# Picks sent to their units by SyncE, the streams' states one in a step, and the step sizes' products in the norm's last steps

## The reference

```
h = rmsnorm(x, ln1_w) * (1 + sc1) + sh1
proj = h @ w_in;  z, xbc, dt, lx, ly, g_ssd, g_lru = split(proj)
xbc = silu(causal_conv(xbc));  dt = softplus(dt + dt_bias)
y, ssd_h_new = ssd_scan(xs, dt, -exp(a_log), bm, cm, h0)     # chunked state space scan
y_ssd = rmsnorm(y * silu(z));  y_lru = rglru(conv(lx)) * gelu(ly)
x = x + g1 * ((sigmoid(g_ssd) * (y_ssd @ w_br_ssd) + sigmoid(g_lru) * (y_lru @ w_br_lru)) @ w_out)
h = rmsnorm(x, ln2_w) * (1 + sc2) + sh2
q = h @ wq;  128 experts per token by two top-16 searches over 128 keys, then a top-16 of the sums
x = x + g2 * sum_k gelu(h . u[e_k]) * g_k * v[e_k]
```

## Time and profile before

| | us |
|---|---|
| median of 3 runs | 4614.37 |
| lowest and highest | 4608.49, 4616.39 |
| the profiled execution: its own time | 4609.44 |
| its span, first to last instruction | 4607.7 |
| mean granted TensorE clock | 0.799 |

### The profile page before, as it was taken

How to read it: one execution, slowest core, us unless ns; L and a number is a source line. 1 busy time by engine, 2 the same in 40 slices (tenths; PEclk the granted TensorE clock), 3 DMA queues, 4 the chain that set the end, 5 groups by cost and what they waited for, 6 DMA issues and landing times. The chain is left out here.

```text
span 4607.7 us, 60395 instructions
## 1 busy us (share of the span) xinstructions
PE 3212.4 (70%) x21986; PEld 1895.2 (41%) x21986; DVE 2825.9 (61%) x6591; ACT 1466.3 (32%) x4657; POOL 1436.5 (31%) x1298
## 2 busy tenths in 40 slices
PE   7899994777777664488999864767777664444443
PEld 4455552445454442254555431445555442121111
DVE  2422058695864587676743696965854587675454
ACT  2224012443622222333722222433622222232222
POOL 0000003333334334323333323334334334344332
PEclk8999996878888776589999875778888786555555
DMA  7333328899999999968999978999999999999998
GB/s 320 142 147 101 101 82 320 343 356 379 417 417 419 419 400 396 413 265 311 382 380 378 366 292 364 395 364 406 418 418 419 420 404 390 421 420 421 421 422 336
DMA packets 279860, 1610.83 MB, mean 350 GB/s; under 512 B 56410, under 2 KB 61328, under 8 KB 112524
## 3 DMA queue, kind: packets, MB, share of 16 engines
q0 software_dynamic: 184320, 1342.26, 71.6%
q1 hardware_dynamic: 65808, 255.49, 14.5%
q10 hardware_dynamic: 29436, 9.24, 0.8%
HBM read 1597.63 MB, written 7.91 MB: 348 GB/s over the span
## 5 line engine op out<-in xcount | busy, mean ns | idle before, releaser
L528 POOL DMA_INDIRECT ring<-in_peer_uv,units x1280 | 1433.3, 1120 | 3136.3 <-PE psum L923 2219.9
L1827 DVE SCALAR_TENSOR_TENSOR ring<-ring,hrow 128x1024 f32<-128x1024 f32 x1280 | 1538.4, 1222 | 890.7 <-DMA ring<-in_peer_uv,units 864.3
L923 PE MATMUL psum<-ring,diag 128*32 128x256 f32 x10240 | 926.0, 495 | 1182.9 <-ACT diag L1292 1181.9
L541 PE MATMUL psum<-hT,wslot 128*128 128x384 f32 (+1 forms) x4224 | 1283.0, 461 | 27.7 <-DMA wslot<-in_w_tiles 24.6
L541 PEld LDWEIGHTS psum<-hT,wslot 128*128 128x128 f32 x4224 | 845.7, 205 | 456.9 <-issue 111.1
L923 PEld LDWEIGHTS psum<-ring,diag 128*32 128x32 f32 x10240 | 322.2, 131 | 1705.1 <-ACT diag L1292 1394.1
L1282 ACT ACTIVATE gel<-hid 128x2 f32<-128x2 f32 x640 | 129.1, 202 | 1935.5 <-DVE ring L1827 1881.0
L541 PE MATMUL psum<-region,wslot 128*128 128x384 f32 (+1 forms) x1536 | 446.8, 446 | 5.5 <-DVE xT L1682 2.2
L541 PEld LDWEIGHTS psum<-region,wslot 128*128 128x128 f32 x1536 | 293.8, 195 | 152.0 <-issue 28.2
L1292 ACT ACTIVATE diag<-pick,wgt 128x32 f32<-128x32 f32 x1280 | 331.7, 306 | 0.0
L1286 ACT ACTIVATE wgt<-gel,units 128x1 f32<-128x1 f32 x1280 | 307.4, 287 | 20.9
(11 more groups left out here) (247 smaller groups left out, 2806.0 us busy)
## 6 DMA issues: line engine op xcount, KB each, us to landing
wslot<-in_w_tiles SPq DMA_DIRECT2D x360, 512.0 KB, 7.7
ring<-in_w_modt SPq DMA_DIRECT2D x24, 2048.0 KB, 9.0
ring<-in_peer_uv,units POOLq DMA_INDIRECT x1280, 13.7
wslot<-in_w_gate SPq DMA_DIRECT2D x32, 128.0 KB, 9.6
region<-in_states_t SPq DMA_DIRECT2D x16, 256.0 KB, 13.2
region<-in_states_n SPq DMA_DIRECT2D x16, 256.0 KB, 10.0
out_new_ssd_sample<-region ACTq DMA_DIRECT2D x16, 256.0 KB, 15.4
xT<-in_x_t SPq DMA_DIRECT2D x1, 2560.0 KB, 8.9
```

The source lines that it names most:

```text
L528: pool.indirect_dma_start(ring[:, n, :], None, table, bass.IndirectOffsetOnAxis(ap=units[:, s % 2, block, 0, quad:quad + 1].bitcast(U32), ...
L541: last = pe.matmul(out, wslot[:, n % SLOTS, k * P:(k + 1) * P], src(k), start=k == 0, stop=k == KT - 1)
L923: last = pe.matmul(psum[c * BLOCK:(c + 1) * BLOCK, block % 2, block // 2 * 256:(block // 2 + 1) * 256], diag[:, n, :], ring[:, n, D + c * ...
L1827: dve.scalar_tensor_tensor(out=ring[:, n, 0:D], in0=ring[:, n, 0:D], scalar=1.0, in1=hrow[:, e % 2, :], op0=ALU.mult, op1=ALU.mult, accum_ ...
```

## The change

SyncE walks the same plan. It issues weight loads up to four tiles past those that the entries so far have used, and issues the picks' DMAs at the entries where ACT did. The last three `states_n` loads stand behind the first three LX tiles. The eight states are added, scaled and written one in a step instead of two. On PE the products of the step sizes for prompt tiles stand in N1's steps 6 to 9, two rows of h in each, as these become `modulated`; those of the streams' tile stay in X0.

```
+                ahead, taken = weights(), 0
+                for e, steps in PLAN:
+                    while n < min(taken + SLOTS, REGIONS * LOADS):
+                        next(ahead)
+                    if e and e[0] < TILES_E and same_group(e[0]) and e[1] == choice_at(e[0]) + 28:
+                        spread(e[0] + 1, 0)
+                    for r, i in steps:
+                        if r < REGIONS:
+                            taken += loads_in(r, i)
+                            if r == 0 and i == BASE[0]["Q"] + 13:
+                                spread(0, 0)
+                            if i == BASE[r]["Q"] + 21:
+                                spread(TILE0[r], passes(TILE0[r]) - 1)
...
-                        if g and j == 4:
-                            states(l)
+                            if g and j == 4:
+                                states(l, range(13))
+                            yield load(tile(l, TZ + j))
...
+                        for j in range(8):
+                            yield load(tile(l, TLX + j))
...
+                            if g and j < 3:
+                                states(l, (13 + j,))
...
+                def spread(s, h):
+                    sp.wait_ge(E["ready"], s + h + 1 if s == 0 else s + 2)
+                    if s >= 2:
+                        sp.wait_ge(E["wgt"], (s - 1) * UNITS)
+                    c = slice(h * length(s), (h + 1) * length(s)) if s == 0 else slice(0, QUADS)
+                    for block in range(BLOCKS):
+                        for r in range(BLOCKS):
+                            sp.dma_start(units[r * BLOCK:(r + 1) * BLOCK, s % 2, block, :, c],
+                                         picked[block * BLOCK:(block + 1) * BLOCK, s % 2, r, :, c]).then_inc(E["spread"], 16)
...
 # PE
+                def steps_of_dt(lay, u, k):
+                    return pe.matmul(bank(7)[:, u * HEADS:(u + 1) * HEADS], hT[:, k, lay.t0 + u * P:lay.t0 + (u + 1) * P],
+                                     wdt[:, k * HEADS:(k + 1) * HEADS], start=k == 0 and u == 0, stop=k == KT - 1, skip_group_check=True)
...
+                    if -6 <= i < -2:
+                        if i == -6:
+                            pe.wait_ge(S["mean"], at("mean", 2 * r))
+                            pe.wait_ge(loaded["wdt"], 16 * (l + 1))
+                        pe.wait_ge(S["modulated"], at("modulated", 2 * r, 2 * i + 13))
+                        for k in (2 * i + 12, 2 * i + 13):
+                            for u in range(lay.nt - lay.sample):
+                                last = steps_of_dt(lay, u, k)
+                        if i == -3 and not lay.sample:
+                            last.then_inc(S["dt_mm"], 1)
...
 # PE, DVE and ACT, the streams' states (9, 10 and 11 are steps of the tile's scan)
-                    if 9 <= i <= 12:
+                    if 9 <= i <= 16:
+                        j = i - 9
...
-                    if s and 10 <= i <= 13:
+                    if s and 10 <= i <= 17:
+                        j = i - 10
...
-                        if 11 <= i <= 14:
+                        if 11 <= i <= 18:
+                            j = i - 11
...
 # ACT
-                    if r == 0 and i == 13:
-                        spread(0, 0)
-                    if i == 21:
-                        spread(s, passes(s) - 1)
...
-                        if p == choice_at(s) + 28:
-                            spread(s + 1, 0)
```

More of the change, by code:

```diff
@@ L163, with loads_in @@
 POS = weight_positions()
+LOADS = 98
+TILE0 = [NT * (r // 2) + FIRST[r % 2] for r in range(REGIONS)]
+def loads_in(r, i):
+    return sum(each for name, count, each in (("X", 10, 1), ("Z", 8, 1), ("LX", 8, 1), ("LRU", 8, 2), ("M", 32, 1), ("OUT", 8, 1), ("Q", 16, 1))
+               if 0 <= i - BASE[r][name] < count)
 PER = {"zeroed": 2, "sampled": 2, "modset": 3, "zscaled": 8, "xfill": 18, "conved": 18, "tapped": 18, "kept": 18, "xth": 10, "silued": 10, "acb": 2, "ea": 2, "seg": 4, "e": 4, "w": 2, "y": 2, "ys": 2,
@@ L431, in small_ones, with states @@
                     sp.dma_start(kT[:], a["keys"].rearrange("p (l i k) -> p l i k", l=DEPTH, i=2)[:, l, :, :]).then_inc(loaded["keys"], 16)
-                def states(l):
+                def states(l, loads):
                     lay = G[1]
-                    for i in range(16):
+                    for i in loads:
                         slot = i % 5
@@ L482, in _ @@
+                for _ in ahead:
+                    pass
             @block.gpsimd
@@ L589, in x_stage @@
                             pe.wait_ge(S["sampled"], at("sampled", l, 0))
-                        pe.wait_ge(S["mean"], at("mean", 2 * r))
-                        pe.wait_ge(loaded["wdt"], 16 * (l + 1))
-                        for u in range(lay.nt):
                             for k in range(KT):
[L594 to L597, removed]
+                                last = steps_of_dt(lay, lay.nt - 1, k)
+                            last.then_inc(S["dt_mm"], 1)
                     if 0 <= i < 10:
@@ L1293, in diagonals @@
                            .then_inc(E["diag"], 1)
-                def spread(s, h):
-                    act.wait_ge(E["ready"], s + h + 1 if s == 0 else s + 2)
-                    if s >= 2:
-                        act.wait_ge(E["wgt"], (s - 1) * UNITS)
-                    c = slice(h * length(s), (h + 1) * length(s)) if s == 0 else slice(0, QUADS)
-                    for block in range(BLOCKS):
-                        for r in range(BLOCKS):
-                            act.dma_start(units[r * BLOCK:(r + 1) * BLOCK, s % 2, block, :, c],
-                                          picked[block * BLOCK:(block + 1) * BLOCK, s % 2, r, :, c]).then_inc(E["spread"], 16)
                 def take_out(o):
```

93 lines of the change are left out of this document (44 added, 49 removed).

## The result

| | us |
|---|---|
| before, median of 4 runs | 4611.43 (4608.39 to 4616.39) |
| after, median of 4 runs | 4584.81 (4583.61 to 4585.75) |
| ratio after/before, 95% interval | 0.9943 (0.993 to 0.9955) |
| after, the profiled execution and its span | 4585.02, 4583.3 |

The change saves 24 to 27 us, 0.6%. The forecast was 4586 us. The sum is right; several of its terms are not, and they cancel, which is in part luck. This part shows where the time came from, place by place.

The account below looks back on a forecast made before the run. Gathers set the pace wherever the DMA engines move 417 to 422 GB/s. Terms -5, -3.7, -4, -14, -3 and +3 sum to -26.7 us, from 4609.4 to 4583 (4588 against the median); forecast 4586 us, its own range 4573 to 4602.

Parts of the forecast that it names:

- The bound: Whole run: gathers set the pace at 417 to 422 GB/s; an edit gains only DMA time given back elsewhere.
- Step sizes in region 2: Region 2's norm and X0: products follow ACT two rows at a time, X0 ends earlier; -5 us.
- Region 0: Region 0's products: PE starts at 42.5 instead of 46.2, passes end at 52.9 instead of 56.6; -3.7 us.
- Regions 1 and 3: Norm and X0 there: 16 of 32 passes move, 3.5 us each, counted 2 us each; -4 us, bounds -7 and +6.
- The picks: Picks leave ACT for SyncE, at tile 0, tile 5 and other sets; -14 us together, bounds -22 and 0.
- 7.5 us for a set is my estimate: SyncE's issue of a set of picks, from five state loads at 0.47 us each, against ACT's 10.5 us.
- the 3 at the start: First half of tile 0's picks: the first gather can start 3 us earlier (0 to 6).
- Weights behind the picks: SyncE's weight loads behind each set of picks: issues and landing fit the cover of 20 to 30 us; 0.
- States in region 1: States one in a step, late loads behind LX tiles; DVE still waits 5 to 10 us; -3 us, bounds -10 and +8.
- States in region 3: State loads behind tile 6's picks, PE waits 10 to 16 us at S11; +8, so +3 with the gain.
- More comes back: Rival, 20%: ring covers S11 in region 3, no DVE wait in region 1, N1 waits free; -47 us, 4567.
- The slower rival: Rival, 10%: weights come late behind the picks, 15 us at each of four sets; +33 us, 4647.

Follow-up runs that it names:

- E1: Kernel before with only the step sizes' products moved into the norm's last steps; 4597.53 us, ratio 0.9974.
- E2: Kernel before with only the picks issued by SyncE along the plan, states two in a step, all loads at Z4; 4598.53 us, ratio 0.9970.
- E4: Changed kernel with the step sizes' products back in X0; 4595.18 us, ratio 0.9965.
- E5: Changed kernel with the first five state loads of a region issued right behind the load of Z3, ahead of tile 6's picks; 4580.53 us, ratio 0.9936.
- E6: Changed kernel with tile 1's picks three plan entries later, behind region 1's last two state loads; 4578.06 us, ratio 0.9929.
- E8: Changed kernel with tile 1's picks three and tile 6's fifteen entries later, behind the last state loads of their region; 4568.67 us, ratio 0.9918.
- E10: E8 with the step sizes' products of regions 1 and 3 back in X0; 4570.63 us, ratio 0.9921.
- E3: Kernel before with only the states one in a step and their last three loads behind LX tiles; 4602.93 us, ratio 0.9988.
- E11: E8 with states two in a step and all 16 loads at Z4, as before; 4577.65 us, ratio 0.9936.
- E12: E9 with each state written as 128 rows of 2 KB, not 1024 of 256 bytes, in other output places; a probe only; 4562.58 us, ratio 0.9898.
- E9: E8 with the first half of tile 0's picks issued half by SyncE and half by ACT; 4567.53 us, ratio 0.9913.

## Why the prediction was right, and where its steps were not

- **The bound.** Reading the price of an edit from the GB/s of its own stretch held: the saturated stretches gave nothing (unit 128 to 384: 14.3 to 15.7), and the dips gave all.
- **Step sizes in region 2: -5, measured -6.5 (E1) to -8.3.** The mechanism is as told, group by group behind ACT, with the pair's sums behind them. The last product ends 3.2 us after ACT's last row, for 2.6. But the terms differ. PE gains 5.4 us up to X0's end, of which 1.8 are X0 at a higher clock, a term that the forecast did not have. X0's start was forecast 14.0 us behind ACT's first row (1961.5 - 1947.5) and came at 15.3: the step that was mis-sized is the pair's sums and the turning, put at about 3 us together, which took 3.5 (1942.9 to 1946.4), and the last product, put 11.3 us behind ACT's first row and measured at 11.8. Without the clock the gain would have been 3.6. E2 to E4, with the old code, gain 0.9 to 1.7 by the lead here too, so of the 6.5 some 5 are left; and of the 8.3 up to unit 464 the last 1.6 are in neither E1, E5, E6 nor E8 (-0.5 to 0.0).
- **Region 0: -3.7, measured 3.5** between ACT's and PE's starts, 4.2 in the lead and 4.0 between the means of the kernels with and without it.
- **Regions 1 and 3: -4, measured about 0 in the changed kernel.** The step that failed is "I count 2 us each": 3.5 us of passes left X0, but the rest of the products, with the pairs' sums now between them, end no sooner. In region 3 X0 starts 14.8 us behind ACT's first row and before 14.6, in region 1 13.5 and 13.3. From unit 656 to 704, which holds region 3's N1, the lead is 26.7 and 27.0. In region 1 four kernels of nine got 3 to 4 us, with the clock at 1.00 in X0 (told with E10); the forecast did not have that either.
- **The picks: -14, measured -14 (E2), by other terms.** The step that failed is "7.5 us for a set is my estimate" (tile 0's halves took 10.3 and 10.8, tile 1's and tile 6's sets 11.8 and 11.4): five state loads in a row were the wrong neighbour for transfers of another form, and ACT's own row, which I had as the bound, was the truth. That takes away the 3 at the start. The second half of tile 0 gave 8 rather than 5, and tile 8 gave 3.4 that I had put among the stretches that hide it. E2's net of 14, by the ratio (its one profiled execution shows 9), even holds a loss of 10 in region 3, an effect of order that I had booked under the states.
- **Weights behind the picks: 0, measured 0.** No wait for w_tiles is left in the waits of the changed kernel.
- **States in region 1: -3.** The lead grew by 2.9 here, but by 5.8 with the picks alone (E2, units 64 to 408), by 3.0 with the states alone (E3), by 2.5 with both (E4) and by 1.6 with neither (E1): beside the picks the states' part brought nothing that shows, and only with the picks behind the states does it (E8 against E11, 3.5 us from unit 96 to 128). The wait foretold was 5 to 10 us and is 17.7: SyncE's 11.8 us of issues and 12 us to landing were added up rightly to 20 and more, but the time until DVE wants the state was put at 10 to 15 us, and it was 6.7 (from 1054.4 to 1061.1).
- **States in region 3: +3 with the gain counted, measured +4.6** (unit 704 to 768). The wait at L759 was foretold at 10 to 16 us and is 13.2; the further 8 us at S13 were 1.8 (PE at 3032.5); that the picks stand in front was read in the order and is the cause (E5 by its failure, E8 by its success).
- **The rivals.** "More comes back" named the right places: without those two waits E8 stands at 4568.7, and this rival was priced at 4567. It did not come to pass because both waits did. That the two numbers are so near is chance: its terms of 7 us for regions 1 and 3 and of 17 for the picks were not measured. The slower rival did not appear.
- **Luck.** The sum is within 2 us of the median because a term of 4 us for regions 1 and 3 and one of 3 for the start brought nothing, while the second half of tile 0 and tile 8 brought 3 each more than forecast, and region 2's clock made up for its lateness.

## What to carry to other kernels

When a queue is given more work, read in the order what now stands behind it, and move the new work behind whatever is wanted sooner: two numbers in SyncE's order brought half as much again as the whole change. Price an issue by the same kind of transfer on any engine, not by another kind on the right engine. And when a repair moves some of the delayed issues forward, as E5 did, ask which one is delayed next before counting the gain.

## What the runs showed of the hardware that I had not expected

- A transfer between SBUF tiles of 32 partitions (4 KB for tile 0's halves, 8 KB for the others) costs SyncE 0.507 to 1.514 us of issue, 0.592 in the median (176 after), and ACT 0.513 to 1.439, 0.612 in the median (176 before); two engines issue such transfers side by side at full pace each (8 in 5.2 and in 5.6 us).
- A store of 256 KB as rows of 256 bytes leaves ACT in 0.38 us in the median of the changed kernel's 16, but with the gathers running at 420 GB/s it can hold it for 12 to 16 us (12.44 at 1031.5 and 16.27 at 3079.6 after). As rows of 2 KB it never did (E12: 0.374 at most, 16 stores, with the gathers at 416 to 420 GB/s). The two landings on record in E12 took 7.5 and 7.8 us, the four in E9 from 5.1 to 27.3.
- Loads of 256 KB in rows of 2 KB did not hold SyncE: the eight behind tile 6's picks stretch over 11.85 us after, but their issues add up to 3.8 us, none over 0.65. The rest of the time SyncE waits, from the sixth on, for a slot that PE has read. The issue of the first five takes 0.43 to 0.65 us each, and 0.43 before.
- The granted clock in X0 of region 2 was 0.65 to 0.79 in the four kernels with all products in X0 and 0.84 to 1.00 in the ten with them in the norm's steps; X0 took 6.8 to 8.3 us and 5.4 to 6.5 us.
